# Hybrid encoder layer on one core: the last sample tile's logits and affinities inside the next tile's product, top-k rounds placed anew, four expert chunks fetched a stage earlier, the lists converted by ACT

## What is computed

```python
x = x + merged @ w_o                                   # output projection
t = rmsnorm(x, norm2_g)
aff = softmax(t @ w_router)                            # 16 experts
gate, idx = top_k(aff.T, cap)                          # cap = 2 * n_tok / 16, for prompt and sample apart
xe = t[idx]
hid = silu(xe @ w_gate[e]) * (xe @ w_up[e])            # e = 0..15, 1024 x 1024 each
out[idx] += (hid @ w_down[e]) * gate                   # scattered back onto x
```

## Time and profile before

| | us |
|---|---|
| Median of 3 runs | 2477.19 (2477.11 to 2478.91) |
| Profiled execution, its own time | 2479.48 |
| Its span | 2477.5 |
| PE busy | 2337.7 (94%) |
| DVE busy | 1209.7 (49%) |
| ACT busy | 913.4 (37%) |
| POOL busy | 476.2 (19%) |

### The profile page before, as it was taken

The page is one execution under the profiler, slowest core; times in us unless marked ns, Lnnn a source line. Parts: engine busy times, 40 slices in busy tenths (PEclk is TensorE's granted clock), DMA queues, the critical chain, the costliest instruction groups (busy, mean ns, idle before and its releaser), DMA issues. The chain is left out here.

```text
span 2477.5 us, 36530 instructions
## 1 busy us (share of the span) xinstructions
PE 2337.7 (94%) x14401; PEld 2051.0 (83%) x14401; DVE 1209.7 (49%) x1752; ACT 913.4 (37%) x1458; POOL 476.2 (19%) x297
## 2 busy tenths in 40 slices
PE   7999989998899999999999999479999999999997
PEld 5877765666788888888878878369999999999997
DVE  6444445545323230000144543757676776667773
ACT  6443443444500011211120033235555554555652
POOL 0011101110200000000000000234454343453442
PEclk9999998999999999999999999679999999999998
DMA  6310000001011112222245454477888887888882
GB/s 192 98 34 18 26 18 18 26 18 43 14 39 36 40 34 77 85 88 83 84 161 166 150 193 148 146 232 257 275 272 277 267 275 248 264 282 277 254 277 51
DMA packets 327844, 343.34 MB, mean 139 GB/s; under 512 B 11664, under 2 KB 308368, under 8 KB 327184
## 3 DMA queue, kind: packets, MB, share of 16 engines
q1 hardware_dynamic: 315024, 309.83, 39.0%
q0 software_dynamic: 12672, 31.46, 4.8%
HBM read 297.22 MB, written 44.04 MB: 138 GB/s over the span
## 5 line engine op out<-in xcount | busy, mean ns | idle before, releaser
L2250 PE MATMUL bank_pair<-tokens_hi_lo,ehi 128*128 128x320 f32 x2048 | 536.4, 348 | 6.0 <-DVE tokens_hi_lo L2087 3.3
L2251 PE MATMUL bank_pair<-tokens_hi_lo,elo 128*128 128x160 f32 x2048 | 484.9, 237 | 0.0
L2006 ACT ACTIVATE ehi<-eraw 128x2048 fp32r<-128x2048 f32 x192 | 364.6, 1907 | 85.5 <-PE bank_pair L2251 66.5
L2251 PEld LDWEIGHTS bank_pair<-tokens_hi_lo,elo 128*128 128x128 f32 x2048 | 394.0, 192 | 0.0
L2250 PEld LDWEIGHTS bank_pair<-tokens_hi_lo,ehi 128*128 128x128 f32 x2048 | 387.2, 189 | 6.5 <-issue 6.5
L2076 DVE TENSOR_TENSOR elo<-eraw,ehi 128x2048 fp32r<-128x2048 f32 x141 | 332.0, 2354 | 25.0 <-ACT ehi L2006 20.8
L1980 POOL TENSOR_TENSOR elo<-eraw,ehi 128x2048 fp32r<-128x2048 f32 x47 | 235.5, 5011 | 380.9 <-ACT ehi L2006 380.8
L2250 PE MATMUL bank_pair<-hidden_hi_lo,ehi 128*128 128x320 f32 x1024 | 265.3, 346 | 0.0
L2251 PE MATMUL bank_pair<-hidden_hi_lo,elo 128*128 128x160 f32 x1024 | 241.3, 236 | 0.0
L1344 PE MATMUL bank_pair<-hT_hi,whi 128*128 128x512 f32 (+1 forms) x576 | 204.0, 354 | 1.2 <-PEq L1136 1.2
L1345 PE MATMUL bank_pair<-hT_lo,whi 128*128 128x512 f32 (+1 forms) x576 | 204.0, 354 | 0.0
(11 more groups left out here) (275 smaller groups left out, 4072.5 us busy)
## 6 DMA issues: line engine op xcount, KB each, us to landing
eraw<-in_w_eg SPq DMA_DIRECT2D x64, 1024.0 KB, 6.8
eraw<-in_w_eu SPq DMA_DIRECT2D x64, 1024.0 KB, 6.4
eraw<-in_w_ed SPq DMA_DIRECT2D x64, 1024.0 KB, 6.0
raw<-in_w_in SPq DMA_DIRECT2D x64, 512.0 KB, 4.1
scratch_g<-sig SPq DMA_DIRECT2D x24, 640.0 KB, 3.5
sig<-scratch_g SPq DMA_DIRECT2D x24, 640.0 KB, 3.9
xt<-in_x SPq DMA_DIRECT2D x10, 512.0 KB, 4.9
scratch_m<-acc SPq DMA_DIRECT2D x8, 640.0 KB, 4.7
```

The lines of the kernel that those rows point to most:

```text
L2006: nc.scalar.activation(ehi[j % NES][:], eraw[j % NER][:], ACT.Copy).then_inc(e_hi, 1)
L2250: nc.tensor.matmul(out, wh, moving[:, k, :], start=(k == 0), stop=False)
L2251: ins = nc.tensor.matmul(out[:, HI], wl, moving[:, k, HI], start=False, stop=(k == KD - 1))
```

## The change

In iteration 8, the last sample tile's (tile 7's) transposes go into the middle of `half(0)`; its logits go between the two halves, and the transpose of its affinities into the middle of `half(1)`. ACT's exponential and DVE's softmax and copy of tile 7 move with them into iteration 8. `SAMPLE_ROUNDS` now has six parts: one round ahead of tile 8's add, one between tile 8's add and its normalisation, three behind that, one behind tile 8's softmax in iteration 9, one behind tile 9's in iteration 10, and nine in the expert block. Four of expert 0's six first chunks are loaded within the projection block, behind SP's loads for tile 5. The list conversions go to ACT, without the offsets `NP_` and `NP_ + HALF_S`, which two operations of the merge now add. And ACT splits the sample rows before it copies the prompt rows.

```diff
--- before.py
+++ after.py
@@ -1631,7 +1631,8 @@
     tk = sem("topk_step")
     d_made = sem("aff_cleared")
     ROUNDS_P, ROUNDS_S = CAP_P // 8, CAP_S // 8
-    SAMPLE_ROUNDS = (range(0, 2), range(2, 5), range(5, 9), range(9, ROUNDS_S))
+    SAMPLE_ROUNDS = (range(0, 1), range(1, 2), range(2, 5), range(5, 6), range(6, 7), range(7, ROUNDS_S))
+    PRELOADED = 4
     tk_done = [1]
@@ -1684,6 +1685,10 @@
             for n in range(2, N4):
                 load(n, n % 2, 16 * (n // 2))
+                if n == N4 // 2:
+                    sp.wait_ge(wo_l, KD)
+                    for c in range(PRELOADED):
+                        sp.dma_start(eraw[c][:], expert_src(0, c)).then_inc(er_loaded[c], 16)
...
@@ -1704,6 +1709,12 @@
                     for k in range(KE, KD):
                         wo_split_hi(act, k)
+            def exponentials(n):
+                act.wait_ge(lg_max, n)
+                wait(act, af_ready, n - 1)
+                nc.scalar.activation(expo[:], bank[4][:, 0:NEXP], ACT.Exp, bias=st2[:, 2:3],
+                                     accum_out=st2[:, 3:4]).then_inc(lg_exp, 1)
+
...
@@ -1726,11 +1739,8 @@
...
+                if one and n != N_S:
+                    exponentials(n)
             stages(act, body)
@@ -1753,16 +1763,34 @@
                 for r in SAMPLE_ROUNDS[part]:
                     topk_round(dve, list_v, list_i, aff_s[:], r)
+            def affinities(n):
+                dve.wait_ge(lg_done, n)
+                wait(dve, lg_exp, n - 1)
+                nc.vector.tensor_reduce(st2[:, 2:3], bank[4][:, 0:NEXP], AX.X, ALU.max,
+                                        negate=True).then_inc(lg_max, 1)
+                dve.wait_ge(lg_exp, n)
+                nc.vector.reciprocal(st2[:, 4:5], st2[:, 3:4]).then_inc(lg_inv, 1)
+                dve.wait_ge(lg_inv, n)
+                wait(dve, af_tr, n - 1)
+                _to, r0 = rows_of(n - 1)
+                nc.vector.tensor_scalar(aff[:, r0:r0 + NEXP], expo[:], st2[:, 4:5], None,
+                                        ALU.mult).then_inc(af_ready, 1)
+
+            def affinities_out(m):
+                dve.wait_ge(af_tr, m + 1)
+                to, r0 = rows_of(m)
+                nc.vector.tensor_copy(to, bank[5][r0:r0 + NEXP, 0:P]).then_inc(af_cp, 1)
+
...
-                if two:
-                    dve.wait_ge(af_tr, n - 1)
-                    to, r0 = rows_of(n - 2)
-                    nc.vector.tensor_copy(to, bank[5][r0:r0 + NEXP, 0:P]).then_inc(af_cp, 1)
-                if n == N4 - 1:
+                if two and n != N_S + 1:
+                    affinities_out(n - 2)
+                if n == N_S:
+                    affinities(n)
+                    affinities_out(n - 1)
                     dve.wait_ge(af_cp, N_S)
                     sample_rounds(0)
                 if now:
@@ -1772,44 +1800,56 @@
...
+                if n == N_S:
+                    sample_rounds(1)
                 if now:
                     dve.wait_ge(x1_rs, 2 * n + 2)
                     nc.vector.scalar_tensor_tensor(tn[h][:], x1[h][:], st2[:, h:h + 1], g2b[:], ALU.mult,
                                                    ALU.mult).then_inc(t_ready, 1)
...
-                if n in (N4 - 1, N4):
-                    sample_rounds(n - (N4 - 1) + 1)
+                if one and n != N_S:
+                    affinities(n)
+                if N_S <= n <= N4:
+                    sample_rounds(n - N_S + 2)
             stages(dve, body)
         @block.tensor
         def _(pe):
+            def affinities_turned(m):
+                pe.wait_ge(af_ready, m + 1)
+                wait(pe, af_cp, m)
+                n_rows = rows_of(m)[1] + NEXP
+                nc.tensor.transpose(bank[5][0:n_rows, 0:P], aff[:, 0:n_rows], ident[:]).then_inc(af_tr, 1)
+
+            def logits(n):
+                if n == 1:
+                    pe.wait_ge(s_c4, 32)
+                pe.wait_ge(t_cp, n)
+                wait(pe, af_ready, n - 1)
+                for k in range(KD):
+                    ins = nc.tensor.matmul(bank[4][:, 0:NEXP], tT[:, k, :], wr[:, k, :], start=(k == 0),
+                                           stop=(k == KD - 1))
+                ins.then_inc(lg_done, 1)
+
             def body(n, h, i, now, one, two):
-                def half(a):
-                    for k in range(KE if n == 0 else 0, KD):
+                def half(a, ks):
+                    for k in ks:
                         if n == 0:
+                            if k < KE:
+                                continue
                             pe.wait_ge(wo_l, k + 1)
                             if k == KL:
                                 pe.wait_ge(mg_l, 1)
                         ins = wo_product(h, a, k)
                     return ins
+                last = n == N_S
+                MID = KD // 2
                 if now:
                     if n > 0:
                         pe.wait_ge(mg_l, n + 1)
                     wait(pe, x1_ready, n - 1)
-                    half(0)
+                    half(0, range(MID if last else KD))
                 if one:
                     pe.wait_ge(t_ready, n)
                     wait(pe, t_cp, n - 1)
@@ -1817,22 +1857,18 @@
...
+                if last:
+                    half(0, range(MID, KD))
+                if two and n != N_S + 1:
+                    affinities_turned(n - 2)
+                if last:
+                    logits(n)
+                    half(1, range(MID))
+                    affinities_turned(n - 1)
                 if now:
-                    half(1).then_inc(mm4, 1)
...
+                    half(1, range(MID if last else 0, KD)).then_inc(mm4, 1)
+                if one and not last:
+                    logits(n)
             stages(pe, body)
@@ -1934,7 +1970,7 @@
...
-            for c in range(NER):
+            for c in range(PRELOADED, NER):
                 sp.dma_start(eraw[c][:], expert_src(0, c)).then_inc(er_loaded[c], 16)
             run_experts(sp, body)
@@ -2062,9 +2098,14 @@
             for j in range(AHEAD):
                 hi(0, j)
+            act.wait_ge(tk, 1 + 3 * (ROUNDS_P + ROUNDS_S))
+            nc.scalar.activation(tok_i[0:NEXP, :], list_i[0:NEXP, :], ACT.Copy)
+            nc.scalar.activation(tok_i[H1:LROWS, :], list_i[H1:LROWS, ::-1], ACT.Copy)
+            nc.scalar.activation(back_v[H1:LROWS, :], list_v[H1:LROWS, ::-1], ACT.Copy).then_inc(lists_ready, 1)
+            for b in range(2):
+                x_split(0, b, 0, 0)
             prompt_copy(0)
-            for b in range(3):
-                x_split(0, b, 0, 0)
+            x_split(0, 2, 0, 0)
...
@@ -2165,12 +2206,8 @@
                 nc.vector.tensor_copy(idx_rep[:, k, :], idx_p[:])
                 ins = nc.vector.tensor_scalar(idx_w[:, k, :], idx_p[:], float(KD), float(k), ALU.mult, ALU.add)
             ins.then_inc(packed, 1)
-            for r in SAMPLE_ROUNDS[3]:
+            for r in SAMPLE_ROUNDS[-1]:
                 topk_round(dve, list_v, list_i, aff_s[:], r)
-            dve.wait_ge(tk, tk_done[0])
-            nc.vector.tensor_scalar(tok_i[0:NEXP, :], list_i[0:NEXP, :], float(NP_), None, ALU.add)
-            nc.vector.tensor_scalar(tok_i[H1:LROWS, :], list_i[H1:LROWS, ::-1], float(NP_ + HALF_S), None, ALU.add)
-            nc.vector.tensor_copy(back_v[H1:LROWS, :], list_v[H1:LROWS, ::-1]).then_inc(lists_ready, 1)
...
@@ -2183,11 +2220,13 @@
             dve.wait_ge(merging, 2)
             va, ia, vb, ib = (merge[:, NEXP * n:NEXP * (n + 1)] for n in range(4))
             nc.vector.tensor_tensor(take[:], va, vb, ALU.is_ge)
-            nc.vector.tensor_tensor(diff[:], ia, ib, ALU.subtract).then_inc(merging, 1)
+            nc.vector.scalar_tensor_tensor(diff[:], ia, -float(HALF_S), ib, ALU.add, ALU.subtract).then_inc(
+                merging, 1)
             dve.wait_ge(merging, 3)
             nc.vector.tensor_tensor(diff[:], diff[:], take[:], ALU.mult).then_inc(merging, 1)
             dve.wait_ge(merging, 4)
-            nc.vector.tensor_tensor(idx_c[0][:], diff[:], ib, ALU.add).then_inc(merging, 1)
+            nc.vector.scalar_tensor_tensor(idx_c[0][:], diff[:], float(NP_ + HALF_S), ib, ALU.add,
+                                           ALU.add).then_inc(merging, 1)
             dve.wait_ge(merging, 5)
             nc.vector.tensor_copy(ig_cur[0][:], idx_c[0][:, 0:1]).then_inc(ig_ready, 1)
             nc.vector.tensor_tensor(gates_c[0][:], va, vb, ALU.max)
```

More of the change, by code:

```diff
@@ L1728, in body @@
                     nc.scalar.activation(st2[:, h:h + 1], st2[:, h:h + 1], ACT.Exp, scale=-0.5).then_inc(x1_rs, 1)
-                if one:
-                    act.wait_ge(lg_max, n)
-                    wait(act, af_ready, n - 1)
-                    nc.scalar.activation(expo[:], bank[4][:, 0:NEXP], ACT.Exp, bias=st2[:, 2:3],
-                                         accum_out=st2[:, 3:4]).then_inc(lg_exp, 1)
+                if one and n != N_S:
+                    exponentials(n)
```

(40 more changed lines are left out.)

## The result

| | before | after |
|---|---|---|
| Median of 6 runs, us | 2477.15 (2476.30 to 2479.36) | 2487.68 (2487.19 to 2489.22) |
| Ratio, 95% interval | | 1.0042 (1.0032 to 1.0052) |
| Profiled execution, its span | 2479.48, 2477.5 | 2487.19, 2485.5 |

The change costs 10.5 us. The forecast was 2474.9 us within 2470.0 to 2484.5, a gain of 2.3 us that it counted as no change: wrong in its sign, and the range did not hold the time either.

A forecast was written before the change was run, and what follows sets the result against it. PE bounds the kernel (94% busy); time returns only where it stands still, chiefly between projection and experts, held by DVE's work before the gather. Terms -3.05 - 2.15 - 1.3 - 0.5 + 4.7 = -2.3 gave 2474.9 us, range 2470 to 2484.5.

The forecast's parts named there:

- the price of the lock: Expert block's start: DVE's packing copies wait for POOL's second product, then go together; +4.7 us, between +0.4 and +13.6.
- Rival A: Same place: POOL wins the lock each time, the 12 copies end with its fourth product; +13.6, 2483.8 us, chance 0.27.
- the preload's cost: Projection stage: four chunk loads ahead of tile 6's load, which lands near 1508 to 1510; cost 0, bound +1.5 us.
- rival C: Projection stage: tile 6's load or tile 8's tokens land late, PE waits; +1 to +2 us, chance within the forecast's 0.35.
- To the cast: From tile 9's add to DVE's cast of the prompt indices in the expert block: 7.85 us shorter.
- tile 8's add: Projection iteration 8: with tile 7's logits and affinity transpose inside it, tile 8's product ends 2.0 us later.
- DVE idle before tile 9's softmax: Projection stage's end: DVE waits for tile 9's logits; about 3 us idle, so three rounds taken out buy only 0.75.
- The two more rounds: Expert block: seven sample top-k rounds become nine, +4.57 us.
- The lists: From the last round to the merge copy: ACT converts the lists, -2.15 us, between -2.4 and -1.55.
- The first split: Before PE's first expert product: ACT splits sample rows before copying prompt rows, -1.3 us, between -1.5 and -1.0.
- the gather: Token-row gather before the experts: preloaded chunks leave it an empty DMA queue, -0.5 us, between 0 and -1.5.
- The forecast without lock and slip: Whole run with no wait of DVE for POOL and no late tile 6: -7.0 us, 2470.2 us.

The follow-up runs named there:

- kernel 6: Changed kernel with chunk loads behind tile 9's load; POOL makes only the low parts of chunks 0 and 1, DVE those of 2 and 3: 2479.79 us.
- Kernel 3: Changed kernel with chunk loads behind tile 9's load and POOL's four differences held until the packing copies are done: 2469.61 us.
- kernel 1: Changed kernel with its four chunk loads moved from behind tile 5's load to behind tile 9's: 2483.89 us.
- kernel 5: Kernel before plus four chunk loads behind tile 5's load, POOL's differences held until the packing copies are done: 2481.70 us.
- kernel 2: Changed kernel without preload, all six chunk loads at the start of the expert block: 2469.67 us.
- kernel 7: As kernel 6, with SP's next chunk loads held until both gathers have landed: 2478.23 us.
- kernel 4: Kernel before with one thing added, four chunk loads behind tile 9's load: 2486.09 us.

## Why the prediction was wrong

**The step that failed first is the price of the lock:** "I take +4.7: the cast's gap of about 0.2 us is longer than the 0.13 that POOL leaves, while the twelve overlap each other". It is +13.4 (14.67 us instead of 1.24 from the cast to the first round). DVE's operations do not keep the lock between them by following each other closely: when the cast lets go, POOL's next product begins, when that ends exactly one copy gets in, and POOL has it again. One operation per product, four products, and kernel 6 with two products has exactly one waiting copy less per product left out. Kernel 3, where POOL is only held back, has none. The flaw was to argue from how DVE's starts overlap when neither side waits. The waiting copies show no such overlap: each ends with its product, and the next waits for the whole of another. And rows of before that showed single meetings could not say who wins next. I had written that much down myself, and still put the most weight on one product out of four.

The Trainium skill (SBUF — State Buffer, "Who interferes with whom") says that copies, casts and tensor_scalar in the two-port mode take the pair shared with GpSimd for a whole instruction, and that issue order decides who blocks. The rows agree, for three kinds: COPY 4.43, COPY 4.53, TENSOR_SCALAR 4.53, each waiting for a whole product. Rival A, which was that rule read instruction by instruction, gave +13.6 for it.

**The second is the preload's cost:** "both fit by 1512.1. PE's margin is 1.7 us: cost 0, bound +1.5". It is +3.7 to +3.9 (the changed kernel against kernel 1, and kernel 5 against before). The rate was right. The DMA view of the changed kernel, 1485 to 1520, GB/s in 40 equal slices:

```profile
GB/s 0 0 0 0 206 393 0 70 140 145 384 405 378 386 378 351 349 346 349 346 350 356 352 369 408 378 395 408 359 342 359 364 310 198 24 6 0 0 206 389
```

At 350 to 400 GB/s the 4 MB of chunks take the 12 us that I gave them. But I let the tile land right behind them, at 1508 to 1510, and it came at 1513.6. Its issue began only at 1499.46: SP's issues ahead of it took 4.23 and 2.85 us where such loads take 0.37 and 0.58 elsewhere (1587.40, 1587.82). The kernel before shows this too: its third to fifth chunk load in a row took SP 1.61, 3.08 and 2.92 us to issue (1592.72 to 1597.50). From 1491 to 1514 the engines moved 7.7 MB, of which 4.2 are the chunks. POOL's three writes of 0.5 MB (issued 1490.92, 1501.62, 1504.68) are 1.6 of them, about 4 us of the engines at that rate; I had seen them, and weighed only whether *they* had slack. The rest belongs to four loads of 0.5 MB that SP issued besides, tile 6's among them. How much of the delay is these bytes and how much the order on the queue, no run separates. And the stall is priced twice: 1.91 us of waiting, then 1.5 us by the matmuls at the 0.50 clock; the whole is 3.7 here. The prediction counted only the wait, and its rival C ("+1 to +2") did so too.

**Everything else held.** To the cast -7.87 against -7.85, with its stages: tile 8's add 15.83 behind tile 7's instead of 13.75, so +2.08 (forecast 2.0); 3.47 us of DVE idle before tile 9's softmax (forecast 3.3); the block's end 7.9 earlier behind tile 9's add, with that stage's slip taken out. The two more rounds +4.59 (+4.57). The lists -2.09 (-2.15), with ACT's copies 0.31, 0.31 and 0.29 long. The first split: ACT's prompt copy to PE took 3.31, now 2.07, -1.24 (-1.3). For the gather I had -0.5 and got -0.2. The forecast without lock and slip was -7.0 us, 2470.2. Kernels 2 and 3 measured 2469.7 and 2469.6 beside a kernel before of 2477.7, which is 1 us more; between tile 3's add and PE's first expert product they gain 6.7 and 6.8.

**What I would do differently in the argument.** Both failed steps took a value from the favourable end of their bounds: +4.7 out of 0.4 to 13.6, and 0 out of 0 to 1.5. The chances (0.27 for A) were not absurd, but A and C were added nowhere: the range stopped at A alone (2484.5), and a run with both is at 2487.7. Two independent costs, each possible, belong in the range as a sum.

One part of the change is not worth its trouble even where it does no harm: the preload, 0.16 us between kernels 2 and 3, while it moves POOL into the packing copies.

## What to carry to other kernels

A string of short DVE copies, casts or tensor_scalars beside back-to-back POOL operations cost here one whole POOL operation of 4.47 us for each of them, up to the number of POOL's; before you let POOL start earlier, look at what DVE has queued there, and hold POOL or give the copies to ACT. Loads that are put ahead of another on a queue have to be reckoned with all that the DMA engines carry in that time, other queues' writes too (here the next load landed 14.1 us after its issue began, instead of 6.9), and a PE stall of 1.9 us cost nearly twice that with the lower clock behind it. When two costs are possible at once, put their sum into the range.

## What the hardware showed beyond that

- The lock alternates, one for one: DVE operations of 0.16 us get in one at a time at the ends of POOL products of 4.47, in five kernels with the same durations (0.62 or 0.63, 4.43, 4.53, 4.53 with four products; 0.62, 4.43 with two).
- The DVE operation need not be large: 16x32 elements are enough, on 16 of the partitions, and a cast from uint32 as well.
- A gather's issue on POOL takes 2.34 instead of 1.02 us beside DVE differences with two SBUF inputs (kernels 6 and 7), and two chunk loads beside the gather delay its rows by another 2.5 us. The Trainium skill (SBUF — State Buffer, "Who interferes with whom") infers that a tensor_tensor leaves the preparation of such DMAs alone; here the issue got longer, and the measured 2.34 decides. In both kernels each of the two issues ends 0.8 to 0.9 us behind the end of one of DVE's differences (kernel 6: 1622.36 behind 1621.44, 1624.49 behind 1623.67), as if it had waited for it. That the reading of the list of rows is what waits was not tried.
- DVE's conversion of a 16x128 uint32 list takes 0.21 us as soon as POOL is idle (kernel 4), and 2.12 to 2.56 where POOL still runs: ACT's conversion (0.31) is only better as long as DVE's has to wait for POOL.
